# Start addresses of the split weight halves and of the split activation tiles, moved in steps of 16 bytes

## What is computed

```
h = x
for i in range(2):
    y = even_mixer(h, ...) if i == 0 else odd_mixer(h, positions, ...)
    h = layer_norm(ALPHA * h + y, ...)
    u = square(relu(h @ mlp_w1[i])) @ mlp_w2[i]          # 1024 -> 4096 -> 1024
    h = layer_norm(ALPHA * h + u, ...)
    h = h + sigmoid(h @ ple_gate_w[i]) * (p[i] @ ple_w[i])
for l in range(2):
    h = h + 0.5 * (silu(n1 @ w_gate) * (n1 @ w_up)) @ w_down   # n1 = rms_norm(h), 1024 -> 2816 -> 1024
    h = h + mixer(rms_norm(h) @ w_in) @ w_out
    h = h + 0.5 * (silu(n2 @ w_gate2) * (n2 @ w_up2)) @ w_down2
out = rms_norm(h)
```

## The kernel before

| columns | stationary | moving | matmuls before |
|---|---|---|---|
| 256 | weights at 0 | activation at 32 | 4,560 |
| 256 | weights at 64 | activation at 32 | 4,512 |
| 256 | weights at 32 | activation at 32 | 1,536 |
| 256 | activation at 32 | weights at 32 | 480 |
| 512 | weights or activation at 32 | the other at 32 | 6,744 |
| 392 | activation at 32 | weights at 32 and at 64 in turn | 96 |

## Time and profile before

### The profile page before, as it was taken

The page is one execution under the profiler, slowest core; times in us unless marked ns, Lnnn a source line. Parts: engine busy times, 40 slices in busy tenths (PEclk is TensorE's granted clock), DMA queues, the critical chain, the costliest instruction groups (busy, mean ns, idle before and its releaser), DMA issues.

```text
span 3239.5 us, 47396 instructions
## 1 busy us (share of the span) xinstructions
PE 3189.8 (98%) x20092; PEld 2852.8 (88%) x20092; DVE 2035.9 (63%) x2889; ACT 1415.4 (44%) x2128; POOL 837.1 (26%) x377
## 2 busy tenths in 40 slices
PE   8999999999999999999999999999999999999998
PEld 7887999988779999889998889999899988889997
DVE  6577755445857444476666637667667566466756
ACT  5354544443635444354443324444445333244542
POOL 1210033320500333202321430232123223312322
PEclk9999999999999999999999999999999999999999
DMA  5211223322203332323322322332323223222322
GB/s 175 82 40 53 97 98 118 104 98 68 70 27 107 102 112 94 125 67 105 130 80 83 123 92 74 106 129 79 105 95 116 96 91 117 78 91 98 125 84 78
DMA packets 223219, 308.95 MB, mean 95 GB/s; under 512 B 7872, under 2 KB 151248, under 8 KB 222752
## 3 DMA queue, kind: packets, MB, share of 16 engines
q1 hardware_dynamic: 219424, 291.41, 27.0%
q0 software_dynamic: 3584, 14.52, 1.3%
HBM read 303.80 MB, written 2.10 MB: 94 GB/s over the span
## 4 chain that ended last, share of the span: by engine, by line
PE 69%; DVE 21%; ACT 6%; issue 3%; DMA 1%; POOL 0%; DVEq 0%; SPq 0%; ACTq 0%
PE bank L609 21%; PE bank L611 21%; PE bank L610 21%; DVE wlo L2141 5%; ACT whi L1349 4%; DVE wraw L2163 2%; DVE raw_w L2163 2%; PE bank L629 1%; DVE ul_w L2351 1%; PE bank L1007 1%; DVE zt L2346 1%; DVE wkk_o L2983 1%; DMA wraw<-in_e_w_in 1%; DVE t_w L2346 1%; DVE gb L2981 1%
## 5 line engine op out<-in xcount | busy, mean ns | idle before, releaser
L3226 POOL TENSOR_TENSOR wlo<-wraw,whi 128x1024 fp32r<-128x1024 f32 (+1 forms) x189 | 492.5, 2610 | 1310.9 <-ACT whi L1349 1310.8
L609 PE MATMUL bank<-xh,whi 128*128 128x256 f32 (+1 forms) x2456 | 719.0, 293 | 15.3 <-DVE xl L2443 7.9
L610 PE MATMUL bank<-xl,whi 128*128 128x256 f32 (+1 forms) x2456 | 713.6, 291 | 0.0
L611 PE MATMUL bank<-xh,wlo 128*128 128x256 f32 (+1 forms) x2456 | 713.5, 291 | 0.0
L1349 ACT ACTIVATE whi<-wraw 128x1024 fp32r<-128x1024 f32 (+2 forms) x399 | 435.0, 1095 | 628.6 <-PE bank L611 478.8
L3226 POOL TENSOR_TENSOR wlo<-raw_w,whi 128x1024 fp32r<-128x1024 f32 x114 | 292.5, 2570 | 839.7 <-ACT whi L1349 839.7
L609 PEld LDWEIGHTS bank<-xh,whi 128*128 128x128 f32 x2456 | 464.0, 189 | 33.8 <-DVE wlo L2141 10.3
L2141 DVE TENSOR_TENSOR wlo<-wraw,whi 128x1024 fp32r<-128x1024 f32 (+1 forms) x210 | 278.0, 1327 | 314.9 <-ACT whi L1349 314.1
L609 PE MATMUL bank<-whi,uh_w 128*128 128x512 f32 x1216 | 474.3, 390 | 0.7 <-DVE ul_w L2772 0.7
L611 PE MATMUL bank<-whi,ul_w 128*128 128x512 f32 x1216 | 473.4, 389 | 0.0
L610 PE MATMUL bank<-wlo,uh_w 128*128 128x512 f32 x1216 | 473.3, 389 | 0.0
(11 more groups left out here) (402 smaller groups left out, 4966.9 us busy)
## 6 DMA issues: line engine op xcount, KB each, us to landing
wraw<-in_w_in SPq DMA_DIRECT2D x26, 1024.0 KB, 5.1
wraw<-in_ffn_w_gate SPq DMA_DIRECT2D x40, 512.0 KB, 4.7
raw_w<-in_ffn_w_gate SPq DMA_DIRECT2D x40, 512.0 KB, 4.6
raw_w<-in_ffn_w_up SPq DMA_DIRECT2D x40, 512.0 KB, 4.7
wraw<-in_ffn_w_up SPq DMA_DIRECT2D x40, 512.0 KB, 4.7
wraw<-in_ffn_w_down SPq DMA_DIRECT2D x20, 1024.0 KB, 5.0
raw_w<-in_ffn_w_down SPq DMA_DIRECT2D x20, 1024.0 KB, 5.0
raw_w<-in_mlp_w SPq DMA_DIRECT2D x19, 1024.0 KB, 5.0
```

The lines of the kernel that those rows point to most:

```text
L609: M.matmul(o, lh, rh, start=start, stop=False, skip_group_check=more)
L610: M.matmul(o, lh, rl, start=False, stop=False, skip_group_check=more)
L611: return M.matmul(o, ll, rh, start=False, stop=stop, skip_group_check=more)
L3226: G.tensor_tensor(lo[:, 0:n], raw[:, 0:n], hi[:, 0:n].bitcast(F), ALU.subtract).then_inc(*k.w_lo.inc(("lo", j)))
```

## The change

No instruction is added, dropped or moved on any engine. Only the byte at which some tiles begin changes:

| tile | before, past a multiple of 128 | after |
|---|---|---|
| halves 0, 1, 2, 3 of `whi` and `wlo` | 32 (in a `Unit`: 0, 64, 0, 64) | 0, 16, 32, 48 for every item |
| `xh`, `xl` | 32, 32 | 0, 16 |
| `ah_w`, `al_w` (sums) | 32, 32 | 32, 48 |
| `uh_w`, `ul_w` (result or gated tile, now two parts of `u`) | 32, 32 | 32, 48 |

The float32 scratch tiles that share the place of `uh_w` and `ul_w` move with them. The raw tiles stay at 32.

```
+STEP = (0, 4, 8, 12)
...
-    k.xh, k.xl = sb("xh", [128, 8, T], R), sb("xl", [128, 8, T], R)
+    sb("x_edge", [128, 24])
+    k.xh, xl = sb("xh", [128, 8, T], R), sb("xl", [128, 8 * T + 8], R)
+    k.xl = xl[:, 4:4 + 8 * T].rearrange("p (f t) -> p f t", t=T)
...
-            s.ah, s.al = tmp("ah", [128, 3, 4, 256], R), tmp("al", [128, 3, 4, 256], R)
-            with nc.sbuf_tensor("u32_w", [128, 2, 8, T], F) as u32:
-                free = [u32[:, 0, :, :], u32[:, 1, :, :]]
-            s.uh, s.ul = tmp("uh", [128, 8, T], R), tmp("ul", [128, 8, T], R)
+            s.ah, al = tmp("ah", [128, 3, 4, 256], R), tmp("al", [128, 3 * 1024 + 32], R)
+            s.al = al[:, 4:4 + 3 * 1024].rearrange("p (a k t) -> p a k t", k=4, t=256)
+            halves = [(a, a + 8 * T) for a in (0, 8 * T + 4)]
+            with nc.sbuf_tensor("u32_w", [128, 16 * T + 8], F) as u32:
+                free = [u32[:, a:b].rearrange("p (f t) -> p f t", t=T) for a, b in halves]
+            u = tmp("u", [128, 16 * T + 8], R)
+            s.uh, s.ul = [u[:, a:b].rearrange("p (f t) -> p f t", t=T) for a, b in halves]
...
-    at = h % 2 * HALF + EDGE
-    if item.unit:
-        at += EDGE if h % 2 else -EDGE
+    at = h % 2 * HALF + STEP[h]
```

## The result

The changed kernel takes 3262.46 us (median of 3 runs, 3261.61 to 3263.1) against 3241.29 us: a ratio of 1.0069, with a 95% interval of 1.0055 to 1.0083. It is slower by 21.2 us. The prediction was 3254.1 us, 12.8 us slower.

What follows compares the result with a forecast made beforehand. PE's matmul stream, busy 3189.8 of 3239.5 us, was taken as the bound. Narrow terms +13.9 (weights stationary) and -1.1 (activation stationary), others 0, sum to +12.8 us: 3254.1 us, 0.4% slower, whole range 3212 to 3280 us.

Steps and rivals of the forecast that it cites:

- Weights stationary, 256 columns: 10,608 narrow matmuls: stationary starts at multiples of 64 take 116.7 ns, those between 120.0; +13.9 us.
- Moving start: All matmuls: moving `xh` from 32 to 0 gains nothing visible, judged by the 392-column product; 0 us.
- Wide matmuls: 6,840 wide matmuls: mixed starts keep about the settled gap of 226.7 ns; 0 us, bounds -22.6 to +45 us.
- loses the settled state: Rival, wide stream: starts changing within groups of three never settle; +22.6 us on top of narrow +12.8, 3276.7 us; chance 0.18.
- Faster rival: Wide and narrow matmuls: side-by-side reads that start apart are cheaper; 3218.7 us, or 3204.7 with narrow gains; chance 0.35.
- Idle time: PE: idle time expected to stay 49.7 us, so longer gaps go into the span one to one.
- Splits: Writes of `whi` and `wlo` by ScalarE, VectorE and GpSimd go to new starts; slack covers any cost, 0 us.

Runs made afterwards that it cites:

- e10: Against the kernel before, only narrow items get weight halves at 0, 32, 16, 48 and `al_w` goes to 48; wide items keep 32: 3242.19 us, ratio 1.0004.
- e2: The changed kernel with the three old lines of `split_views`, so only the activation tiles move against the kernel before: 3261.35 us, ratio 1.0060.
- e5: The kernel before with 128 unused bytes ahead of `xh`, keeping every start modulo 128: 3272.53 us, ratio 1.0101.
- e11: Against the kernel before, wide weight halves and all activations begin at 16 instead of 32, with 256 bytes taken out of `lo_gap`: 3260.31 us, ratio 1.0061.
- e12: Against the kernel before, activation tiles go 64 bytes on, weights stay, and 256 bytes are taken out of `lo_gap`: 3279.39 us, ratio 1.0118.
- e8: Against the kernel before, the low activation tiles `xl`, `al_w`, `ul_w` go from 32 to 48: 3254.76 us, ratio 1.0044.
- e7: Against the kernel before, the 1,536 narrow matmuls with both operands at 32 get weights at 0 and 64: 3240.28 us, ratio 0.9999.
- e3: Against the kernel before, all operands move by 32 bytes, split tiles are longer, and `xh`, `xl` stand ahead of `wlo1`: 3265.59 us, ratio 1.0076.
- e6: Against the kernel before, 256 unused bytes go ahead of the activations and 256 leave `lo_gap`; of the operands only `wlo1` moves: 3241.06 us, ratio 1.0001.

## Why the prediction was right, and where it was wrong

The sign and the range (3212 to 3280 us) held, and 21.2 us is 1.7 times the forecast of 12.8. That was luck: the mechanism of the forecast was not the one at work. Two of its terms were wrong, in opposite directions (the narrow one by 8.8 us too much, the wide one by 25.6 us too little), the idle time took back 7.5 us, and so the sum came out near.

*Weights stationary, 256 columns: +13.9 us.* Wrong. All narrow gaps together rose by 4.0 us, and e10 has that rise alone without a time that can be measured. The step that failed is "a stationary operand that starts at a multiple of 64 is cheap, one that starts between is dear". The three rows were right, but they had one thing in common, the moving operand at 32. With `xh` at 0 (and `xl` at 16), half 2 at 32 takes 117.9 ns instead of 119.8, and half 0 at 0 takes 118.1 instead of 116.7: the stationary operand's own start alone doesn't set the gap. The trace before had no row with another moving start for 256 columns, and I took three points on one line for a rule.

*Moving start: 0 us.* Near in its sum, without a ground. In e2, where the activations alone move, the narrow gaps go from 117.96 to 118.07 ns, 1.2 us in all; e2's 1.0060 comes from wide matmuls, most of them with the moved activation stationary. But single pairings do change with the moving start, as half 2 above shows. The 392-column rows could not bear that weight: their mean gap varies by no more than 2.2 ns in all fourteen kernels (177.8 to 180.0), so they are blind to what moves the 512-column stream by 5.

*Wide matmuls: 0 us, bounds -22.6 to +45.* Wrong as a value, right as bounds: +25.6 us. This is near the rival "loses the settled state", priced at +22.6 us from half of the surplus of the earlier trace rows; the measured mean surplus is 3.9 ns where it took 3.3. The prediction gave it 0.18, and put its price on top of a narrow term that is hardly there. It had that the short gap is lost, but not why: it blamed starts that change within a group of three, and in e5, e11 and e12 neither operand's start changes modulo 256 within a wide stretch beside `u` or `x`, and the gap is still 230.0 to 233.3 ns. What stood against it ("those rows repeat exactly too, so some state is found for mixed starts") is even true, but what is found in these runs is mostly slower: 230.0, 231.1, 232.2 and 233.3 ns. I should have asked what they cost, not whether they exist.

*Why the wide stream was not looked at closely.* It had a single row with a single pair of starts, and 6,840 matmuls. A term with one row and a slope of 6.8 us per ns deserved the widest thought; I gave it to the three narrow rows because they differed. And the prediction read starts modulo 128, the unit in which the diff and the kernel speak. The change's own 96 bytes of `x_edge` move `x` by 96 and not by -32; e5 shows what the missing 128 cost.

*Faster rival: starts apart are better.* It has a narrow truth (a mean of 117.3 ns in e8 and e11, and 114.4 ns for one small pairing in e12) and is reversed for the wide stream, which weighs more.

*One price for every address.* The Trainium skill, in TensorE: Matmul & The Clock Gate, section Back-to-back issue gap, gives its formula as the gap of a single matmul by itself and names no address; by it the two kernels would take one time, 3241.3 us. The traces disagree: with the same instructions the mean gap of 512 columns runs from 227.2 to 233.0 ns in this study. For a stream of weight loads with their matmuls, such as this one, that section of the Trainium skill has about 131 ns for 512 columns, and no long stretch here is near that either: the shortest long ones have 226.7 ns. The prediction's step from there, that TensorE's "own two reads do meet", is an inference; the runs show that the gap depends on where both operands start, and nothing of the reads themselves.

*Idle time: unchanged.* Wrong by 7.5 us, downwards, and e7 shows the same exchange in the other direction. "Next to no idle time" (49.7 us) was right for what bounds the kernel and not for the size of a difference: it can take a part of a difference, 27% here (7.5 of 28.0). That share is no constant: in e5 it is 7.9 of 41.1 us, and in e12 2.6 of 41.6.

*Splits: 0 us.* Right: busy times and counts of ScalarE, VectorE and GpSimd agree within 0.2%, and PE's wait for `wlo` on VectorE, 1.8 us before, is 2.2 us.

**What stays open.** Why the gap of 226.7 ns is held at 160 past a multiple of 256 for both operands and not at 144 (e11), which of the slower rhythms a stream falls into, and whether other starts with a multiple of 256 between them would reach it. e3's pairs with a distance of 0, both at 128, had 229.2 ns beside `u` and beside `x`, but stood between pairs 128 apart and so can't say. e2's two stretches with equal addresses show that something besides the operands' addresses selects the rhythm, and e2 beside e8 that it isn't the order of the banks. That it is the instant at which the stretch begins is my guess; no run separates it from what the other engines do at that time. The earlier trace rows speak against these for the narrow stream; for the wide one nothing was tried. No version tried is faster than the kernel before by more than the measurement tells.

## What to carry to other kernels

When TensorE is 98% busy, check where the two operands of the most frequent matmul start, each and relative to each other, modulo 256 bytes and not just modulo the unit that the code uses, before and after anything that moves a tile, an unused pad included: 128 bytes of padding cost 1% here. Equal starts are not enough (e11), so measure the gap again. Read the gap from start to start over a long stretch, in several stretches, since a mean over all of them can hide two rhythms. And when one term of a sum has one row and most of the instructions, put the range there, not where the rows differ.

## What the runs showed of the hardware

- Where the starts stay the same through a long stretch, 512-column float32r matmuls run at one of several rhythms that hold for the whole stretch: 226.7, 230.0, 231.1, 232.2 or 233.3 ns, at a mean granted clock of 0.99 and more. 512 columns at the level of 2.4 GHz are 213.3 ns of that.
- With the starts of the kernel before, the distance of the operands counts modulo 256 bytes, as far as tried: 232.3 ns and more at 128 (e5), no difference at 256 (e6, low weights of two halves). An equal start of both is not enough: at 144 past a multiple of 256 no long stretch with moving weights is under 230.0 ns (e11).
- With the starts of the kernel before, all 31 long stretches are at 226.7 to 227.6 ns. With the stationary tile of one matmul in three 16 bytes off, 22 of 30 stretches run at 232.2 ns (e8), some of them for 192 matmuls; in e2 this happens at the same operand addresses as in a stretch at 226.8 ns.
- At a granted clock of 0.50 wide matmuls start 425 ns apart (seven of them in the kernel before).
- For 256 columns the best pairing seen is another one: 114.4 ns with weights moving at 32 and the activation stationary at 96, against 119.8 ns with both at 32.
